# First half's up projection by one level of Strassen, with the output-projection tiles between its steps

## The reference

```python
    merged = gates[..., :D_MODEL] * ya + gates[..., D_MODEL:] * yb
    x = x + rmsnorm(merged @ w_o, g_post_mix)

    h2 = rmsnorm(x, g_pre_mlp)
    f = jnp.square(jax.nn.relu(h2 @ w_up)) @ w_down
    x = x + rmsnorm(f, g_post_mlp)
```

## Time and profile before

| | us |
|---|---|
| median of 3 runs | 961.05 |
| lowest, highest | 960.05, 986.2 |
| the profiled execution | 960.17 |
| its span on the slowest core, core 5 | 959.1 |
| spans of the eight cores | 954.3 to 959.1 |

### The profile page before, as it was taken

One profiled execution on the slowest core, in us unless ns is written; L12 is line 12 of the kernel. 1 busy time (PEld: TensorE's weight loads), 2 busy tenths in 40 slices (PEclk: granted clock), 3 DMA queues, 4 the chain that ended last, 5 costly groups with the idle time before them and its releaser, 6 DMA issues.

```text
span 959.1 us, 15642 instructions; the slowest of 8 cores (954.3 to 959.1 us)
## 1 busy us (share of the span) xinstructions
PE 938.4 (98%) x5158; PEld 463.5 (48%) x5158; DVE 640.3 (67%) x1017; ACT 354.2 (37%) x707; POOL 51.4 (5%) x99
## 2 busy tenths in 40 slices
PE   6899999999999999999999999999999999999997
PEld 4744544444455455455544444444444545544443
DVE  2568886885677777678735655670778887662687
ACT  4344332222433444333334444422023656731032
POOL 2031000000000000000000000000000000000000
PEclk7799999999999999999999999999999999999999
DMA  9999689859889998755227775375692973363683
GB/s 226 256 186 196 132 178 178 165 132 155 152 180 201 192 201 184 119 147 122 78 44 165 169 182 112 86 247 153 163 259 86 165 134 102 102 198 101 188 286 150
DMA packets 70687, 155.13 MB, mean 162 GB/s; under 512 B 22480, under 2 KB 41168, under 8 KB 68304
## 3 DMA queue, kind: packets, MB, share of 16 engines
q0 software_dynamic: 13104, 57.15, 36.1%
q1 hardware_dynamic: 56064, 92.49, 32.7%
q10 hardware_dynamic: 1440, 4.49, 1.2%
HBM read 173.11 MB, written 33.69 MB: 216 GB/s over the span
## 4 chain that ended last, share of the span: by engine, by line
PE 91%; DVE 3%; DMA 2%; issue 2%; ACT 1%; POOL 0%; DVEq 0%; ACTq 0%; POOLq 0%; SPq 0%
PE PS L144 90%; DVE AR L164 2%; DMA AR<-w_a 2%; DVE AR L174 1%; PE PS L148 1%; DMA AR<-wd_d 1%; ACT AR L161 1%; POOL AR L129 0%; ACT WPG L161 0%; DVEq L229 0%; DVE STAT L1002 0%; DVE AR L169 0%; ACT STAT L161 0%; DVE STAT L553 0%; POOL AR L514 0%
## 5 line engine op out<-in xcount | busy, mean ns | idle before, releaser
L144 PE MATMUL PS<-AR 128*128 128x512 bf16 (+1 forms) x4920 | 915.7, 348 | 8.0 <-DMA AR<-w_a 5.1
L144 PEld LDWEIGHTS PS<-AR 128*128 128x128 bf16 x4920 | 444.8, 99 | 468.7 <-issue 12.8
L164 DVE TENSOR_TENSOR AR<-AR 128x512 bf16<-128x512 f32 (+13 forms) x353 | 263.7, 778 | 52.2 <-ACT AR L161 34.2
L164 DVE TENSOR_TENSOR AR<-PS,AR 128x512 f32<-128x512 f32 (+1 forms) x235 | 145.3, 642 | 128.8 <-PE PS L144 96.0
L161 ACT ACTIVATE AR<-PS 128x512 f32<-128x512 f32 (+2 forms) x217 | 126.7, 606 | 237.8 <-PE PS L144 205.7
L161 ACT ACTIVATE AR<-AR 128x1024 bf16<-128x1024 f32 (+4 forms) x123 | 93.5, 766 | 145.9 <-DVE AR L164 122.7
L161 ACT ACTIVATE AR<-PS,CS 128x512 f32<-128x512 f32 (+1 forms) x80 | 48.9, 621 | 76.8 <-PE PS L144 64.0
L174 DVE SCALAR_TENSOR_TENSOR AR<-AR,CS 128x512 f32<-128x512 f32 (+1 forms) x80 | 53.7, 671 | 29.8 <-ACT AR L161 13.2
L161 ACT ACTIVATE AR<-AR,CS 128x512 f32<-128x512 f32 (+1 forms) x40 | 26.3, 658 | 98.0 <-DVE AR L164 80.2
L174 DVE SCALAR_TENSOR_TENSOR AR<-AR,STAT 128x1024 bf16<-128x1024 f32 (+2 forms) x35 | 43.8, 1254 | 4.2 <-DVE STAT L451 1.4
L174 DVE SCALAR_TENSOR_TENSOR AR<-AR 128x512 bf16<-128x512 f32 (+4 forms) x52 | 30.5, 587 | 5.6
(11 more groups left out here) (45 smaller groups left out, 130.7 us busy)
## 6 DMA issues: line engine op xcount, KB each, us to landing
AR<-wd_d SPq DMA_DIRECT2D x56, 512.0 KB, 5.7
AR<-x_p SPq DMA_DIRECT2D x32, 512.0 KB, 7.9
AR<-w_up POOLq DMA_DIRECT2D x16, 1024.0 KB, 11.2
wd_d<-AR SPq DMA_DIRECT2D x16, 896.0 KB, 8.7
AR<-w_m POOLq DMA_DIRECT2D x16, 768.0 KB, 9.6
x_d<-AR SPq DMA_DIRECT2D x17, 512.0 KB, 4.3
AR<-x_d SPq DMA_DIRECT2D x17, 512.0 KB, 9.6
AR<-w_dn POOLq DMA_DIRECT2D x16, 512.0 KB, 10.3
```

The costliest lines, as they stand in the source:

```text
L144: return self.add("pe", lambda e: e.matmul(out, lhsT, rhs, start=start, stop=stop, skip_group_check=skip), reads=[lhsT, rhs], writes=[out] ...
L164: return self.add(eng, lambda e: e.tensor_tensor(out, in0, in1, op), reads=[in0, in1], writes=[out], name=name)
```

## The change

Half 0's up projection uses the same `up_block` as half 1, now with `half` as an argument: 7 products instead of 8, thus 448 matmuls of 128x512 where 512 were. There are 32 steps instead of 64. The nine tiles stand in `S_STEPS`, by the number of the step in the stage (4 x block + s): the tile's matmuls and its `sq_mix` at the end of step t, `rstd`, `mixn`, `x1`, the store and `sq_x1` at the end of step t + 1, `hn` and the transpose at the end of t + 2. The pair of banks 6 and 7 is kept for them, and a block uses the six others. Block 0's sums of h and of weights are made in the last seven steps of the merge stage before; the four weight sums of later blocks in s1 (wu7), s2 (wu6, and wu25 of the next block in two halves) and s3 (wu1 of the next block). The buffers that `cu` writes are two for a block of half 0. Loads of `w_up` for half 0 come in halves with a lead of 6 steps; the planner tries 540 times, and its fixed regions and with them all places change.

```diff
 class Arena:
-    TRIALS = 220
+    TRIALS = 540
...
         def s_mm(i):
             l = i * 128 - HBASE[0 if i < 8 else 1]
-            b2 = bank2()
+            b2 = bank2() if i < 8 else 6
...
-        def s_b1(i):
+        s_ss = {}
+
+        def s_sq(i):
+            ss = s_ss[i] = stat()
+            P.act(JUNK_S, pair(s_bank[i]), AF.Square, accum_out=ss, name="sq_mix")
+            P.act(ss, ss, AF.Sqrt, bias=cs(C_EPS), scale=1.0 / D, name="sqrt")
+
+        def s_sum(i):
             b2 = s_bank.pop(i)
             pm = pair(b2)
-            ss = stat()
-            P.act(JUNK_S, pm, AF.Square, accum_out=ss, name="sq_mix")
-            rstd_from(ss)
+            ss = s_ss.pop(i)
+            P.add("dve", lambda e: e.reciprocal(ss, ss), reads=[ss], writes=[ss], name="rstd")
             P.stt("dve", MT, pm, ss, GPM, ALU.mult, ALU.mult, name="mixn")
...
+        S_STEPS = (1, 4, 6, 9, 12, 14, 17, 20, 22)
...
-                loads[("up", half, b)] = dict(n=8192, lead=6 if half else 16)
...
+                        loads[("up", 0, b, fh)] = dict(n=4096, lead=6, cost=6)
...
         for n_, i in enumerate(range(8, NT)):
-            s0 = 2 + 6 * n_
-            s_at.setdefault(s0, []).append((True, lambda i=i: (s_mm(i), s_b1(i))))
-            s_at.setdefault(s0 + 2, []).append((False, lambda i=i: s_b2(i)))
+            t_ = S_STEPS[n_]
+            s_at.setdefault(t_, []).append((True, lambda i=i: (s_mm(i), s_sq(i))))
+            s_at.setdefault(t_ + 1, []).append((False, lambda i=i: (s_sum(i), s_sq2(i))))
+            s_at.setdefault(t_ + 2, []).append((False, lambda i=i: s_hn(i)))
...
             def final(where, pr, fh, t, eng):
-                c = arv(W.off[("uc", rot("ucb", 3))], F32, [512])
+                c = arv(W.off[("uc", rot("ucb", 3)) if half else ("vc", b, rot("vcb", 2))], F32, [512])
                 P.tt("dve", c, PS[:, st[where, pr], :], st["r", pr], ALU.add, name="cu")
...
-                if b < 7:
-                    wsum(b + 1, 0)
-                    wsum(b + 1, 1)
+                if half == 0:
+                    wsum(0, b, 3)
+                elif b < 7:
+                    wsum(1, b + 1, 0)
+                    wsum(1, b + 1, 1)
...
+                if half == 0:
+                    wsum(0, b, 2)
+                    if b < 7:
+                        wsum(0, b + 1, 0)
+                    return
...
+                if half == 0 and b < 7:
+                    wsum(0, b + 1, 1)
...
+                    def f(fn=fn, bg=bg, n=n):
+                        if b == 0 and n == 0:
+                            held.update((6, 7))
+                        fn()
+                        for _, g in bg:
+                            g()
+                        if b == 7 and n == 3:
+                            held.difference_update((6, 7))
...
+        b_steps = {n_b - 7: [b_last]}
+        for at, fn, w in ([(n_b - a, lambda n=n: hsum(0, n), [("th", t)] if t is not None else [])
+                           for a, n, t in ((6, 1, 1), (5, 6, 0), (4, 7, 2), (3, 3, None), (3, 4, None))] +
+                          [(n_b - a, lambda n=n: wsum(0, 0, n), [("us", 0, n), ("up", 0, 0, 0), ("up", 0, 0, 1)]) for a, n in ((2, 0), (1, 1))]):
```

More of the change, by code:

```diff
@@ L917, in build_program @@
         RLS = RL + [WPG[:, :, :, :].rearrange("p a b c -> p (a b c)")[:, 0:1024].bitcast(F32)]
+        S_STEPS = (1, 4, 6, 9, 12, 14, 17, 20, 22)
         for half in range(2):
             for b in range(8):
-                loads[("up", half, b)] = dict(n=8192, lead=6 if half else 16)
-        FORD = [f for b in range(8) for f in (2 * b, 2 * b + 1, 2 * b + 16, 2 * b + 17)]
+                if half:
+                    loads[("up", 1, b)] = dict(n=8192, lead=6)
+                else:
+                    for fh in range(2):
+                        loads[("up", 0, b, fh)] = dict(n=4096, lead=6, cost=6)
         for i in range(4):
@@ L966, in build_program @@
                 for q in range(4):
-                    loads[("dn", half, p, q)] = dict(n=4096, lead=10 if p == 4 else 7)
+                    loads[("dn", half, p, q)] = dict(n=4096, lead=(10 if half else 6) if p == 4 else 7)
         def evict(dst, b, how):
@@ L1066, in wsum, with up_off, us_off @@
+        def up_off(half, b, fh):
+            return W.off[("up", 1, b)] + 4096 * fh if half else W.off[("up", 0, b, fh)]
+        def us_off(half, b, n):
+            return O_US[b % 2] + (0, 4096, 6144, 8192)[n] if half else W.off[("us", b, n)]
+        def wsum(half, b, n):
+            r0, r1 = (arv(up_off(half, b, fh), BF16, [2, 2, 512]) for fh in range(2))
+            out = arv(us_off(half, b, n), BF16, [2 if n else 4, 512])
             if n == 0:
-                P.tt("dve", out[:, 0:4, :], raw[:, :, 0, :], raw[:, :, 1, :], ALU.add, name="wu25")
+                for fh, r in enumerate((r0, r1)):
+                    P.tt("dve", out[:, 2 * fh:2 * fh + 2, :], r[:, :, 0, :], r[:, :, 1, :], ALU.add, name="wu25")
@@ L1075, in up_block @@
-        def up_block(b, actT):
+                P.tt("dve", out, r0[:, :, 1, :], r1[:, :, 1, :], ALU.subtract, name="wu7")
+        def up_block(half, b, actT):
             st = {}
@@ L1114, in s0 @@
                     prod(5, pr, "Y", True)
-                    st["r", pr] = arv(W.off[("ur", rot("urb", 4))], F32, [512])
+                    st["r", pr] = arv(W.off[("ur", rot("urb", 4)) if half else ("vr", b, pr)], F32, [512])
                     P.copy("act", st["r", pr], PS[:, st["X", pr], :], name="m2")
@@ L1158, in s3 @@
             def s3():
-                if b % 2 == 0:
+                if half and b % 2 == 0:
                     down_scale(0, 4 + b // 2)
@@ L1180, in build_program @@
             actT = arv(O_A, BF16, [32, tn])
-            for f in range(32 if half == 0 else 0):
-                for ui, (c0, n) in enumerate(ugs):
-                    bg = s_at.get(2 * f + ui, [])
-                    def fn(half=half, f=f, c0=c0, n=n, t0=t0, ui=ui, bg=bg, actT=actT):
-                        if f == 0 and ui == 1:
-                            b_last()
-                        up_unit(half, f, c0, n, t0, actT)
-                        for _, g in bg:
-                            g()
-                    step([("up", half, f // 4)] + (O_KEYS if any(x for x, _ in bg) else []), fn)
+            for b in range(8):
+                up_block(half, b, actT)
             if half == 0:
```

109 lines of the change are left out of this document (67 added, 42 removed).

## The result

| | before | after |
|---|---|---|
| median, us | 960.55 (4 runs) | 980.8 (4 runs) |
| lowest, highest | 958.96, 986.2 | 979.98, 983.23 |
| profiled execution, us | 960.17 | 983.23 |
| span of core 5, the slowest | 959.1 | 981.9 |
| spans of the eight cores | 954.3 to 959.1 | 967.5 to 981.9 |

The ratio is 1.0221, interval [1.0193, 1.0248]: slower by 2.2% (that it is more than 2% is not certain), 12 us above the forecast of 969 and just outside its range of 952 to 979.

A forecast was written before the change was run, and what follows sets the result against it. TensorE, busy 98% of the span, was taken as the bound: 960.2 - 13.8 (fewer matmuls) + 20.2 (waits) + 1.7 (clock) = 968.3, and 969 as the runs' median is 0.9 higher; range 952 to 979.

The forecast's parts named there:

- The gain: In the first half's up projection, 64 fewer matmuls at 0.2155 us take 13.8 us off TensorE's path.
- The walk through the queues: Behind blocks 1, 3 and 5, TensorE waits for wu1 (1.7 us), then an m2 copy: 5.4 us each, 16.2 in all.
- the copy's part: Second wait of each pair: product 4 waits for ScalarE's m2 copy, queued behind the square of x1; 3.6 us.
- The start's wait: At the stage's start, block 0's weight sum wu25 stands behind the last merge unit on VectorE: 1.7 us.
- block 0's 0.7: In block 0, a sqrt table load ahead of the S2 pairs makes three S3 products wait: 0.9 us forecast.
- The 1.4 for blocks 6 and 7: Block 6's S3 arrives before wu7, 1.0 us, and block 7's S1 before its wu1, 0.4: 1.4 us.
- the rows' 0.625: Measured time in us of each of ScalarE's four chained final operations, kept over the skill's estimate of 0.52.
- the two milder rivals: Changed stage: waits partly overlap, 956 us (951 to 961, chance 0.16); or nothing waits but the start, 949 (below 951, 0.09).
- one short fall: TensorE's clock in the changed stage falls only once, costing 1.7 us, within bounds of 0 to 10.
- the rival of 977: Each of the three long waits brings a clock fall: 977 us; above 976, shared with late loads, chance 0.13.
- the squeezed loads at nothing: In the earlier merge stage, loads asked for two steps (14.6 us) ahead land in 7.4 to 9.8: no cost.
- the load the prediction doubted: Last pair of up weights, loaded only three steps ahead, can hold VectorE by a microsecond or two, harming no tile.

The follow-up runs named there:

- e4: e1 with the final sums of the Y banks written over the sum r, so no cu waits for a buffer: 962.84 us, 1.0027.
- e10: e1 with the edits of e3, e4 and e6, and block 0's weight sums issued ahead of the last two merge units: 951.72 us, 0.9902.
- e3: e1 with the square of x1, for tiles behind an odd block's S2, issued a step later, behind the m2 copies: 964.14 us, 1.0043.
- e9: e1 with 60 unused matmuls filling TensorE's waits in blocks 2, 4 and 6: cores 0 to 3 took 962.6 to 966.3 us.
- e11: The same kernel as e9, run again for its time: 970.29 us, 1.01.
- e1: The changed kernel with one w_dn load and one w_m load put back in their old order: 974.13 us, 1.0143.
- e5: e1 with every output-projection tile and its sums issued one step earlier: cores 0 to 3 took 959.1 to 963.5 us.
- e6: e1 with the next block's weight sum wu1 issued ahead of the four finals of S3: cores 0 to 3 took 965.0 to 968.8 us.
- e2: The kernel before the change, with only one w_dn load put behind a w_m load: 961.6 us, 1.0033.

## Why the prediction was wrong

**What held.** The gain: 64 matmuls, 141.4 less 127.6, is 13.8 us. The walk through the queues: 20.2 us of waits forecast, 18.2 to 19.1 measured, at the three places and of the two kinds named. Its links, from the earlier trace rows, held one by one: square of x1 1.32 behind x1 (545.40 to 546.72), the copy 1.44 behind that (1.5), TensorE 0.92 behind the copy (0.83). wu1 was later than walked (2.1 to 2.3, forecast 1.7), the copy's part about 0.3 earlier (3.3, forecast 3.6; 2.0 at core 5's third boundary, where product 1's 8 matmuls took 2.99 us at half clock instead of 1.89 and so hid a part). The start's wait, 2.11, stood at 1.7, and block 0's 0.7 at 0.9. The 1.4 for blocks 6 and 7 did not come: behind the long third pair no wait over 0.3 us is left (the one for wu7 shows in e4, on four cores, and in e10). That is most of what the sum was too high by. ScalarE's four operations took 2.58 us, as in the rows (2.59), so the rows' 0.625 was the right choice for the sum. The prediction's estimate of 0.52 from the Trainium skill, "ScalarE: Activation LUTs", section "What ACT_TABLE_LOAD costs", fits only those that don't read the one before: in this chain a relu starts 0.54 behind a square, but a square, which reads its relu's result, 0.70 behind it. But the stage, which the forecast had 6 us longer than before (8 with its fall of the clock), became 12.6 to 14.7 longer. Against e3 and e4, which each took away one link, and e10, which took all, the two milder rivals fall: nothing was swallowed.

**Step that failed: the clock.** "The gap here is surrounded by dense matmuls ... so I take one short fall, 1.7." It fell at all three boundaries on every core, 20.5 us at half clock in the stage (on three cores the start's fall among them), 8.1 to 9.7 us lost. The bound was right (0 to 10, from the earlier trace rows) and the value was taken from its wrong end: in the only row that priced it, 3.3 us of idle time before 38.38, the clock fell, and "dense work around it" was a reason without a row. Three falls were the rival of 977. By the Trainium skill, "TensorE: Matmul & The Clock Gate", section "What's actually happening", activity lifts the throttle and its lack brings it back; by that, as the prediction said, each wait could bring a fall. The runs agree: three falls of three on each core of after, none at the filled waits of e9 and e11.

**Step that failed: the squeezed loads at nothing.** "Those loads land in 7.4 to 9.8 there": a landing time from its issue was set against the lead in steps, but the issue itself waits. POOL issues in the order of the program, and a merge weight whose buffer came free only at 369.28 held a down load behind it; it then landed in 15.4 us, in company of three other loads. The lead in a plan counts from the step at which a buffer is free, and the queue's other loads were not read. This was worth some 7 us (after less e1), 3.3 to 5.8 of wait on seven of the cores (core 1 had none, and its span was 967.5) and the rest in clock. It is not the load the prediction doubted, and it hit VectorE first, where TensorE's sums stood behind.

The sum with the measured terms, core 5: 959.1 - 13.8 + 19.1 + 9.4 + 8.0 = 981.8, span 981.9 (9.4 is the rest of 9.7 less the 0.3 that before has too). With the waits alone it would have been 964.4; the two failed steps are 15.7 of the 17.4 us from there (9.4 less the 1.7 taken, and 8.0).

**What stays open.** When a single wait brings a fall is not settled. It can: the start's wait of 2.1 to 2.3 us did on three of eight cores of after and on one of e1, and that of 1.9 us on two of e4. With waits of 2.6 to 3.1 us one at a time (e4) the clock fell at none or two of three by core, with 2.8 to 2.9 (e5) at one to four of four, and e10's single 1.6 brought none. The same wait in the same kernel brings a fall on one core and none on another, so its length alone does not decide, and the runs show no size from which it is certain. Nor was it tried what the place of the merge weight's buffer does alone.

## What to carry to other kernels

Utilisation of 90% in the engines that serve TensorE says little: with in-order queues, find the instruction that waits for another engine (here a square for x1) and ask what that TensorE needs is queued behind it. Price waits of 2 us and more on TensorE that come in pairs, as here, at about one and a half times their length (18.2 to 19.1 us of waits in after, 8.1 to 9.7 more lost), since the clock can fall with them, also amid dense work; single ones cost between nothing and that. For a re-planned load, read what stands ahead of it in its queue and when that one's buffer comes free, not only how long it takes to land. And an idle time has two ends: removing one of two waits in a row may only lengthen the other (e6).

## What the runs showed of the hardware that was not expected

- The granted clock fell from 1.00 to 0.50 in or behind pairs of waits of 2.0 to 3.4 us with 8 matmuls between them, at 24 of 24 places (three on each of eight cores of after), with 24 to 36 us of matmuls without a wait ahead. 60 matmuls of no use in those waits made e9's stage 4.3 us shorter.
- Half clock costs at most half of its time, and less where part of it passes in a wait: 20.5 us at half clock cost 8.1 to 9.7 us in after.
- A 512 KB load behind another in POOL's queue landed in 15.4 us (after, core 5), 12.9 (e2, core 5), where the profile's median for `w_dn` in after is 11.8.
